# The prompt's RG-LRU: four column blocks in flight, roots in pairs, scans two blocks behind the gates

## The reference

```python
def rglru_dir(xc, w_a, b_a, w_i, b_i, lam, h0, reverse):
    ...
    r = jax.nn.sigmoid(blockdiag(xf, w_a.astype(jnp.float32)) + b_a.astype(jnp.float32))
    ig = jax.nn.sigmoid(blockdiag(xf, w_i.astype(jnp.float32)) + b_i.astype(jnp.float32))
    log_a = -LRU_C * r * jax.nn.softplus(-lam.astype(jnp.float32))
    a = jnp.exp(log_a)
    bterm = jnp.sqrt(-jnp.expm1(2.0 * log_a)) * ig * xf
    bterm = bterm.at[:, 0].add(a[:, 0] * h0.astype(jnp.float32))
    _, h = lax.associative_scan(_lin_combine, (a, bterm), axis=1)
```

## Time and profile before

| | |
|---|---|
| runs | 2457.35, 2460.59, 2462.61 us; median 2460.59 |
| profiled execution | span 2458.3 us; no other time is given for it |
| busy | PE 1778.0 us (72%), DVE 1873.6 (76%), ACT 514.3 (21%), POOL 1037.4 (42%) |
| ACT table loads | 50, of 1283 ns each, 64.2 us |
| DMA | 753.43 MB, mean 306 GB/s |
| granted TensorE clock | 0.860 of full speed, mean |
| prompt's recurrence | about 70 to 158 us |

### The profile page before, as it was taken

How to read it: one execution, slowest core, us unless ns; L and a number is a source line. 1 busy time by engine, 2 the same in 40 slices (tenths; PEclk the granted TensorE clock), 3 DMA queues, 4 the chain that set the end, 5 groups by cost and what they waited for, 6 DMA issues and landing times.

```text
span 2458.3 us, 20346 instructions
## 1 busy us (share of the span) xinstructions
PE 1778.0 (72%) x6013; PEld 1073.5 (44%) x6013; DVE 1873.6 (76%) x3933; ACT 514.3 (21%) x1283; POOL 1037.4 (42%) x1028
## 2 busy tenths in 40 slices
PE   7799889889887989891334666689999996000185
PEld 3578744444356438451012333556666664000032
DVE  2451588756789466889999999888687987999955
ACT  0563116440024000110004655710000000000111
POOL 0000000115534342443774776334344446777674
PEclk9899999899999999996566877899999998555599
DMA  9785772349955695866998999589999999999997
GB/s 279 250 274 193 233 231 87 113 135 319 353 182 180 215 330 177 288 250 211 384 410 285 390 411 404 200 300 411 414 411 414 411 411 411 410 408 406 364 404 304
DMA packets 296873, 753.43 MB, mean 306 GB/s; under 512 B 21502, under 2 KB 141102, under 8 KB 296244
## 3 DMA queue, kind: packets, MB, share of 16 engines
q0 software_dynamic: 147456, 536.94, 57.3%
q1 hardware_dynamic: 149308, 215.20, 25.0%
HBM read 740.72 MB, written 11.33 MB: 306 GB/s over the span
## 4 chain that ended last, share of the span: by engine, by line
DVE 37%; PE 29%; DMA 16%; POOL 8%; issue 6%; ACT 2%; DVEq 0%; SPq 0%; ACTq 0%; POOLq 0%
PE bank L788 12%; PE pair L788 6%; DVE big L1552 5%; DVE attn L1552 4%; DMA ring_more<-in_peer_u_dram,eidx 4%; DMA attn<-in_peer_u_dram,eidx 4%; DVE work L1552 3%; PE bank L971 3%; POOL work L2118 2%; DVE ring_more L1552 2%; POOL attn L2118 2%; PE bank L761 2%; POOL big L2118 2%; DMA attn<-in_peer_v_dram,eidx 2%; PE bank L1019 1%
## 5 line engine op out<-in xcount | busy, mean ns | idle before, releaser
L1019 PE MATMUL bank<-big,work 128*128 128x512 f32 x176 | 110.6, 767 | 369.4 <-ACT work L1091 266.3
L788 PE MATMUL pair<-big 128*128 128x128 f32 (+1 forms) x1280 | 361.8, 440 | 9.1 <-DVEq L1421 6.2
L2118 POOL DMA_INDIRECT h_all<-in_peer_u_dram,eidx x109 | 122.0, 1119 | 577.9 <-DVEq L1987 352.6
L788 PE MATMUL bank<-big 128*128 128x512 f32 (+1 forms) x1056 | 310.9, 453 | 34.4 <-DVEq L1421 22.7
L1064 PE MATMUL bank<-h_all,big 128*128 128x512 f32 x608 | 266.8, 595 | 4.6 <-DMA h_all<-in_peer_v_dram 4.6
L788 PEld LDWEIGHTS pair<-big 128*128 128x128 f32 x1280 | 197.3, 194 | 160.9 <-issue 158.6
L788 PEld LDWEIGHTS bank<-big 128*128 128x128 f32 x1056 | 169.2, 199 | 172.4 <-issue 165.0
L2118 POOL DMA_INDIRECT attn<-in_peer_u_dram,eidx x166 | 163.1, 983 | 165.5 <-DVE dots L1552 97.9
L1019 PEld LDWEIGHTS bank<-big,work 128*128 128x128 f32 x176 | 38.1, 235 | 427.0 <-issue 394.9
L1552 DVE CUSTOM_DVE_ANT_0 attn<-attn,pair 128x1024 f32<-128x1024 f32 x166 | 199.5, 1219 | 25.3 <-DMA attn<-in_peer_u_dram,eidx 23.0
L1064 PEld LDWEIGHTS bank<-h_all,big 128*128 128x128 f32 x608 | 180.5, 297 | 86.7 <-DMA h_all<-in_peer_v_dram 5.4
(11 more groups left out here) (311 smaller groups left out, 3172.7 us busy)
## 6 DMA issues: line engine op xcount, KB each, us to landing
big<-in_w_in_dram SPq DMA_DIRECT2D x44, 1024.0 KB, 6.5
h_all<-in_peer_v_dram SPq DMA_DIRECT2D x76, 512.0 KB, 6.8
big<-in_w_ada_dram SPq DMA_DIRECT2D x24, 1024.0 KB, 8.1
big<-in_peer_w_q_dram SPq DMA_DIRECT2D x16, 1024.0 KB, 5.6
gf_row<-in_peer_v_dram SPq DMA_DIRECT2D x26, 512.0 KB, 6.8
work<-in_peer_v_dram SPq DMA_DIRECT2D x26, 512.0 KB, 6.8
big<-in_w_rnn_o_dram SPq DMA_DIRECT2D x8, 1024.0 KB, 7.9
big<-in_w_attn_o_dram SPq DMA_DIRECT2D x8, 1024.0 KB, 6.4
```

The source lines that it names most:

```text
L788: last = nc.tensor.matmul(u[:, 0:n], w[:, k, col:col + P], src[:, k, 0:n], start=(k == 0), stop=(k == KD - 1))
L1019: last = nc.tensor.matmul(psum[i][:, :], diag[:, (n - 1) % DIAGS, :], ring[r][:, i * 512:(i + 1) * 512], start=(k == first_by_tensor[c]), ...
L2118: g.indirect_dma_start(dst, None, ins["peer_" + table][0], bass.IndirectOffsetOnAxis(ap=eidx[:, c, k:k + 1], axis=0)).then_inc(landed, 16)
```

## The change

For the prompt, blocks now rotate through four places of a row (`j % 4`), and ACT's block j waits for the scan of block j-4. ACT does the roots of blocks j-1 and j together after every odd block. DVE's scan becomes a function and runs two blocks behind: turn j does the gate step of block j and the scan of block j-2 (`LAG`), and the last two scans follow the loop. For the latents the order is as before (`LAG` 0, roots block by block).

```diff
--- before.py
+++ after.py
@@ -376,7 +376,7 @@
 
         def lru_rows(ph, j):
 
-            c0 = (j % 2) * P if ph == 0 else 0
+            c0 = (j % 4) * P if ph == 0 else 0
             return ([wk(2 + 2 * i + d)[:, c0:c0 + TOK[ph]] for d in range(2)] for i in range(5))
 
         sm_pair = [wk(4 * i, 4).rearrange("p (h n) -> p h n", h=G) for i in range(2)]
@@ -1171,9 +1171,9 @@
                     if ph and j:
 
                         act.wait_ge(lru_done, B)
-                    if ph == 0 and j >= 2:
-
-                        act.wait_ge(lru_done, B - 1)
+                    if ph == 0 and j >= 4:
+
+                        act.wait_ge(lru_done, B - 3)
                     for d in range(2):
                         u = full((ph, "gate", j, 2 * d))
                         run(lt[d][:, 0:N], u[:, 0:N], ACT.Tanh, scale=0.5,
@@ -1194,9 +1194,11 @@
                         if ph == 0:
                             gelu_square(j + 1)
                         gelu_tanh(j + 1)
-                    for d in range(2):
-                        act.wait_ge(w_ready, 2 * B + d + 1)
-                        run(le[d][:, 0:N], le[d][:, 0:N], ACT.Sqrt, scale=0.25).then_inc(root_ready, 1)
+                    for i in [j] if ph else [j - 1, j] if j % 2 else []:
+                        _, _, le, _, _ = lru_rows(ph, i)
+                        for d in range(2):
+                            act.wait_ge(w_ready, 2 * (LB * ph + i) + d + 1)
+                            run(le[d][:, 0:N], le[d][:, 0:N], ACT.Sqrt, scale=0.25).then_inc(root_ready, 1)
                 end_stage()
 
 
@@ -1794,24 +1796,9 @@
                         rope((ph, "k", i), kT[:, i, 0:N], final_row)
                     if ph == 0:
                         add_bias(ada_lru[j])
-                conv(0)
-                gelu_out(0)
-                for j in range(LB):
+                def scan(j):
                     B = LB * ph + j
                     lt, la, le, lth, lti = lru_rows(ph, j)
-                    if j + 1 < LB:
-                        conv(j + 1)
-                    y = xc[j % 2][:, 0:N]
-                    for d in range(2):
-                        dve.wait_ge(e2_ready, 2 * B + d + 1)
-
-                        V.scalar_tensor_tensor(le[d][:, 0:N], le[d][:, 0:N], 1.0, lth[d][:, 0:N],
-                                               ALU.add, ALU.mult).then_inc(w_ready, 1)
-                        mark(V.scalar_tensor_tensor(lti[d][:, 0:N], lti[d][:, 0:N], 1.0, y, ALU.add, ALU.mult))
-                    serve(1)
-                    if j + 1 < LB:
-                        gelu_out(j + 1)
-                    chain.wait()
                     for d in range(2):
                         dve.wait_ge(root_ready, 2 * B + d + 1)
                         link(V.tensor_tensor(lti[d][:, 0:N], lti[d][:, 0:N], le[d][:, 0:N], ALU.mult))
@@ -1827,7 +1814,31 @@
                     f = featT[:, j, 0:N]
                     link(V.scalar_tensor_tensor(f, lt[0][:, 0:N], 0.5, f, ALU.mult, ALU.mult))
                     dve.drain().then_inc(lru_done, 1)
+
+                LAG = 0 if ph else 2
+                conv(0)
+                gelu_out(0)
+                for j in range(LB):
+                    B = LB * ph + j
+                    lt, la, le, lth, lti = lru_rows(ph, j)
+                    if j + 1 < LB:
+                        conv(j + 1)
+                    y = xc[j % 2][:, 0:N]
+                    for d in range(2):
+                        dve.wait_ge(e2_ready, 2 * B + d + 1)
+
+                        V.scalar_tensor_tensor(le[d][:, 0:N], le[d][:, 0:N], 1.0, lth[d][:, 0:N],
+                                               ALU.add, ALU.mult).then_inc(w_ready, 1)
+                        mark(V.scalar_tensor_tensor(lti[d][:, 0:N], lti[d][:, 0:N], 1.0, y, ALU.add, ALU.mult))
                     serve(1)
+                    if j + 1 < LB:
+                        gelu_out(j + 1)
+                    chain.wait()
+                    if j >= LAG:
+                        scan(j - LAG)
+                    serve(1)
+                for j in range(LB - LAG, LB):
+                    scan(j)
                 end_stage()
 
                 def merge(a, o, j0):
```

More of the change, by code:

```diff
@@ L1796, in gelu_out @@
                         add_bias(ada_lru[j])
+                def scan(j):
+                    B = LB * ph + j
+                    lt, la, le, lth, lti = lru_rows(ph, j)
+                    for d in range(2):
+                        dve.wait_ge(root_ready, 2 * B + d + 1)
+                        link(V.tensor_tensor(lti[d][:, 0:N], lti[d][:, 0:N], le[d][:, 0:N], ALU.mult))
+                        h0 = 0.0 if ph == 0 else vcols[:, V_SF + d * KD + j:V_SF + d * KD + j + 1]
+                        rev = slice(None, None, -1) if d else slice(None)
+                        a_, b_, o_ = (t_[:, 0:N][:, rev] for t_ in (la[d], lti[d], lt[d]))
+                        link(V.tensor_tensor_scan(o_, a_, b_, h0, ALU.mult, ALU.add))
+                    if ph == 0:
+                        V.tensor_copy(state[:, j:j + 1], lt[0][:, N - 1:N]).then_inc(state_ready, 1)
+                        V.tensor_copy(state[:, LB + j:LB + j + 1], lt[1][:, 0:1]).then_inc(state_ready, 1)
+                        dve.wait_ge(state_ready, 2 * j + 2)
+                    link(V.tensor_tensor(lt[0][:, 0:N], lt[0][:, 0:N], lt[1][:, 0:N], ALU.add))
+                    f = featT[:, j, 0:N]
+                    link(V.scalar_tensor_tensor(f, lt[0][:, 0:N], 0.5, f, ALU.mult, ALU.mult))
+                    dve.drain().then_inc(lru_done, 1)
+                LAG = 0 if ph else 2
                 conv(0)
```

## The result

The changed kernel took 2467.22 us in the median of 9 runs (2461.10 to 2472.69), the kernel before, beside it on the same chip, 2462.61 in 9 (2457.35 to 2464.10): 1.0026 of the time before, 95% interval 1.0014 to 1.0037. It is slower, by 6.2 us as a difference of means. The forecast was 2464.0 us and "no change that can be told": the time lies inside its range, but the change can be told, and it is slower.

The account below looks back on a forecast made before the run. It took a loop of waits (odd block's product, SP, weights, even block) as the bound, and DVE for the stage's end. With -0.2 inside +1.9, 1.9 + 1.5 = +3.4 on 2460.6 gave 2464.0 us, range 2459.5 to 2467.5.

Parts of the forecast that it names:

- no change that can be told: Whole kernel: +3.4 us lies within the 0.2%, 4.9 us, that a measurement cannot tell from no change.
- Scans two blocks later: Stage's end: three scans after DVE's last gate step delay PE's output product from 158.00 to 159.92 us, +1.9 us.
- PE's longer wait: Stage's end: PE waits 3.65 us instead of 1.52, then runs at a lowered clock, +1.5 us, bounds 0 and 1.7.
- The argument's other leg: Trace evidence for the clock term: after a 2.02 us wait the next 16 matmuls took 2.02 us, so no harm.
- a clock that stays low: Rival, chance 0.13: at the first output products after the barrier, 8 us at half rate lose 4 us; 2466.5 us.
- Bank waits: PE's AdaLN products wait for ACT's tanh, 0.8 us in 4 waits; fewer table loads save block 5's, -0.2 us.
- The loop: Inside the recurrence: weight waits cover the saved table loads; even blocks' products still start near 89.5, 110.6 and 130.6 us.
- The sum: Whole kernel: -0.2 inside the +1.9, then 1.9 + 1.5 = +3.4 us, giving 2464.0 us; chance 0.53.
- The loads on the path: Rival, chance 0.04: ACT's table loads lie on the path and all 8 are won, 10.3 us; 2450.3 us.

Follow-up runs that it names:

- e3: Changed kernel with 14 more matmuls, results unused, on PE between the merge gates and the barrier; 1.0029 of the time of the kernel before, +7.5 us.
- e2: Changed kernel, but DVE does the scans of blocks 3 and 4 in turn 5 and block 5's in turn 6, leaving two for the end; 1.0013, +4.1 us.
- e9: Kernel before, but PE waits for the gelu branch's weights only ahead of the gelu product, not already ahead of the input product; 0.9969, -6.7 us.
- e10: Changed kernel with 48 written idle waits (24 instructions) on DVE ahead of the recurrence's first convolution; 1.0009 of the kernel before, +2.9 us.
- e11: Kernel before with 204 written idle waits (102 instructions) on DVE ahead of the recurrence's first convolution; 1.0012, +3.9 us.
- e1: Changed kernel, but ACT does the roots block by block again; four places and scans two blocks behind stay; 1.0040 of the kernel before, +10.4 us.
- e7: Changed kernel, unaltered, timed once more beside the kernel before; 1.0023, +6.6 us.
- e13: Changed kernel with PE's gelu-weight wait moved to just ahead of the gelu product, plus 48 written idle waits on DVE; 0.9991 of the kernel before, 2459.93 us.

## Why the prediction was right or wrong

- *Scans two blocks later, +1.9 us*: right, step by step. 12.40 - 10.47 = 1.93 us. (The prediction's own working, from gates that it put 0.2 us earlier, has 12.59 us from the last gates to the product.) The tanh without a load, the exponentials, three scans without idle time and the 0.25 us to PE all stand where they were put, counted from the last gates. The whole place lies 4.7 us later in the trace (152.24 against 147.53), 1.7 us of it ahead of the loop and 3.0 in it.
- *PE's longer wait, +1.5 us*: right. PE waits 3.42 us where 3.65 was put, and 32 matmuls in 5.44 us instead of 3.81 is 1.6. The e3 filler held the clock, so the wait is its cause. The argument's other leg, that after 2.02 us the next 16 matmuls took their 2.02, is weaker than it looked: e2 lost as much after 2.04 us. The rival of a clock that stays low did not come: behind the first 32 matmuls the granted clock is 1.00 again (168.60 to 172.00 us of after).
- *Bank waits, -0.2 us*: of the four, two are left, of 0.20 us. Right, and lost among the rest.
- *The loop*: wrong, and this is **the step that failed**. "Inside the loop their cover is the wait for weights" priced the change there at the bank waits alone and let the even blocks start as before. Two things were missing. The wait was read as one for the input product's weights; it is for the gelu branch's, whose last part sets the moment (e9). And the cover was taken as fixed, as no DMA of the program moves; but DVE's instructions come by DMA too, and with DVE's work put off one of their packets fell into the load. Worked out from the trace: 0.8 us of wait (2.42 - 1.63) and 1.5 us of clock (3.53 - 2.02), some 2.3 us; in the time, e10 and e11 have 3.7 and 3.9, with the reserve made there.
- *The sum*: 1.9 + 1.6 + 2.3 = 5.8 us, against 6.2 and 6.6 measured. The forecast's 3.4 is near what e10, with the packet out of the way, shows: 2.9. With standard errors of about 1 us, and with e1 and e3 off by 2 and 3 us from their own sums, that agreement is no proof of each term; the places in the traces are.
- *"No change that can be told"*: fell with the missing term, and the bound of 4.9 us was too wide for it: in 9 runs each the interval was 0.1% either way.
- *The loads on the path* (rival): excluded. ACT has 8 fewer and the loop gained nothing from it: e1, with all 50, takes 80.39 us from the first input product to the last gates, after 80.49. What e1 shows is where they do count: 2.05 us at the end, where no other product covers them.

The Trainium skill states both halves of the missing term. "DMA: Bandwidth & Descriptors" ("Why a DMA increments its semaphore by 16 and not by 1") says that the parts of a load finish independently and only all 16 mean that it has landed; the trace agrees (e7: 15 parts by 5.46 us, the last at 6.39). "Runtime: NRT & Kernel Launch" ("Instruction fetch mechanics") says that each sequencer fetches its next page by DMA while it executes the current one, and that the cost is mostly hidden. For DVE the trace agrees: at the packet of 129.4 us in after it stood idle for 2.03 us, and what ended that was ACT at 130.34 us. The price was paid by PE, through the load among whose packets it went out.

## What to carry to other kernels

Before an engine is unloaded, find the instruction that the waiting engine waits for to the tile and the part: here a wait for two tiles, the second of them not needed yet, cost 6.7 us (e9), and all of the change's work was beside it. Work that is pushed back in a loop comes together at its end, where the next stage waits: price that first, and with it the clock that a longer wait loses. When a small change moves the time by a few microseconds where nothing of it should, look for instruction packets in the loads that are waited for, and test it with idle instructions before believing in a mechanism.

## What the runs showed that was not expected

- DVE's program comes in packets of 8 KB, 115 to 137 recorded instructions apart in this stage; one such packet (0.38 us) among 1 MB loads made the last of 16 parts come 0.6 to 1.0 us later.
- In all 14 traces of this stage, after each of PE's waits of 2.32 us and more before an input or output product the next 32 matmuls took 5.2 to 6.1 us, and after each of 1.49 to 1.85 us 3.81. From 1.98 to 2.27 us both came out: 5.44 us after 2.04 (e2), 3.81 after 2.11 (after).
- Idle instructions on an engine with nothing to do moved the whole kernel's time by some 4 us, up or down (e10, e11, e13); the traces place about 2.2 us of that in block 6's weights in e10 and e11, and 0.6 in the stage in e13.
